# Conditioning weights: scaled in place on ScalarE, added on VectorE in operations of 2048, 1024 and 512 elements

## What is computed

```
def adaln(c, w, b):                       # w: 1024 x 6144, one per layer of the second network
    m = jax.nn.silu(c) @ w + b
    return [t[:, None, :] for t in jnp.split(m, 6, axis=-1)]
...
shift1, scale1, gate1, shift2, scale2, gate2 = adaln(c, ada_w[i], ada_b[i])
h = x * (1.0 + scale1) + shift1
```

```
g, u = jnp.split(h @ w_up, [D_FF], axis=-1)      # D_FF = 2816
g = depthwise_conv_centered(g, ffn_conv_w, ffn_conv_b)   # 3 taps
x = x + (silu(g) * u) @ w_down                   # first network
```

## Time and profile before

| what | value |
|---|---|
| median of 3 runs | 2414.7 us (2414.57 to 2418.11) |
| the profiled execution | 2417.73 us, its span 2416.0 us |
| granted PE clock, mean | 0.998 of 2.4 GHz |
| PE busy | 2392.8 us (99% of the span) |
| DVE busy | 1589.2 us (66%) |
| ACT busy | 714.3 us (30%) |
| POOL busy | 154.6 us (6%) |
| chain that ended last | PE 94%, DVE 4%, DMA 1%, issue 1% |

### The profile page before, as it was taken

One profiled execution on the slowest core, in us unless ns is written; L12 is line 12 of the kernel. 1 busy time (PEld: TensorE's weight loads), 2 busy tenths in 40 slices (PEclk: granted clock), 3 DMA queues, 4 the chain that ended last, 5 costly groups with the idle time before them and its releaser, 6 DMA issues.

```text
span 2416.0 us, 41407 instructions
## 1 busy us (share of the span) xinstructions
PE 2392.8 (99%) x17196; PEld 2180.2 (90%) x17196; DVE 1589.2 (66%) x3245; ACT 714.3 (30%) x1436; POOL 154.6 (6%) x268
## 2 busy tenths in 40 slices
PE   9999999999999999999999999999999999999998
PEld 7879999987899998999998899997889999889998
DVE  6653887566289837688744489954456984327983
ACT  3451210144312121433132233223423331443321
POOL 2000100000021000001000032021000000000000
PEclk9999999999999999999999999999999999999999
DMA  7935985574399746589454399743334555335552
GB/s 220 239 94 180 337 305 188 151 188 114 105 337 314 239 155 183 185 314 310 155 174 136 107 344 313 235 152 120 108 120 149 166 167 168 120 105 170 162 166 97
DMA packets 403269, 458.36 MB, mean 190 GB/s; under 512 B 50751, under 2 KB 374776, under 8 KB 403084
## 3 DMA queue, kind: packets, MB, share of 16 engines
q1 hardware_dynamic: 370098, 340.53, 45.2%
q0 software_dynamic: 29936, 112.73, 12.8%
q10 hardware_dynamic: 3050, 2.46, 0.4%
HBM read 451.48 MB, written 1.29 MB: 187 GB/s over the span
## 4 chain that ended last, share of the span: by engine, by line
PE 94%; DVE 4%; DMA 1%; issue 1%; ACT 0%; POOL 0%; DVEq 0%; SPq 0%; POOLq 0%; ACTq 0%
PE job_bank L994 39%; PE job_bank L1070 27%; PE job_bank L1049 11%; PE mix_bank L1049 4%; PE job_bank L1539 4%; PE mix_bank L1486 1%; PE job_bank L1514 1%; PE mix_bank L1458 1%; DVE sb_arena L2908 1%; PE mix_bank L1500 1%; PE mix_bank L1605 1%; PE mix_bank L1025 0%; PE mix_bank L1830 0%; PE job_bank L1262 0%; DVE sb_arena L2952 0%
## 5 line engine op out<-in xcount | busy, mean ns | idle before, releaser
L994 PE MATMUL job_bank<-sb_h,sb_ring 128*128 128x256 f32 x3616 | 807.1, 380 | 0.4 <-DVE sb_h L3186 0.4
L994 PEld LDWEIGHTS job_bank<-sb_h,sb_ring 128*128 128x128 f32 x3616 | 674.4, 189 | 98.9 <-issue 8.1
L2908 DVE SCALAR_TENSOR_TENSOR sb_arena<-sb_arena,sb_c_act 128x512 f32<-128x512 f32 x336 | 253.0, 753 | 10.6
L3015 DVE SCALAR_TENSOR_TENSOR sb_arena<-sb_arena,sb_par 128x256 f32<-128x256 f32 x440 | 204.4, 506 | 8.8 <-ACT sb_arena L2071 4.9
L1049 PE MATMUL job_bank<-sb_h,sb_ring 128*128 128x128 f32 x1600 | 184.1, 275 | 0.9 <-ACT sb_h L2374 0.9
L1049 PEld LDWEIGHTS job_bank<-sb_h,sb_ring 128*128 128x128 f32 x1600 | 181.2, 192 | 1.3 <-issue 1.1
L1070 PE MATMUL job_bank<-sb_t,sb_ring 128*128 128x128 f32 x1248 | 165.5, 275 | 0.0
L2071 ACT ACTIVATE sb_arena<-sb_arena,sb_par 128x256 f32<-128x256 f32 x220 | 120.2, 593 | 122.4 <-DVE sb_arena L2983 121.1
L1070 PE MATMUL job_bank<-sb_h,sb_ring 128*128 128x128 f32 x1152 | 152.8, 276 | 0.0
L1070 PEld LDWEIGHTS job_bank<-sb_t,sb_ring 128*128 128x128 f32 x1248 | 152.2, 192 | 0.0
L1070 PEld LDWEIGHTS job_bank<-sb_h,sb_ring 128*128 128x128 f32 x1152 | 144.3, 192 | 6.1 <-issue 3.3
(11 more groups left out here) (511 smaller groups left out, 3242.3 us busy)
## 6 DMA issues: line engine op xcount, KB each, us to landing
sb_arena<-in_ada_w POOLq DMA_DIRECT2D x96, 1024.0 KB, 7.4
sb_ring<-in_ffn_w_up SPq DMA_DIRECT2D x88, 1024.0 KB, 5.2
sb_ring<-in_w_up SPq DMA_DIRECT2D x44, 1024.0 KB, 6.4
sb_ring<-in_ffn_w_down SPq DMA_DIRECT2D x32, 1024.0 KB, 5.1
sb_ring<-in_w_in SPq DMA_DIRECT2D x24, 1024.0 KB, 6.2
sb_ring<-in_w_down SPq DMA_DIRECT2D x16, 1024.0 KB, 5.3
sb_ring<-in_hg_w_in SPq DMA_DIRECT2D x16, 1024.0 KB, 5.5
sb_ring<-in_ml_w_up SPq DMA_DIRECT2D x16, 1024.0 KB, 5.5
```

Source lines behind the costliest of these rows:

```text
L994: mm = pe.matmul(o, st, mv, start=(k0 + k == 0 and t == 0), stop=(k0 + k == kn - 1), skip_group_check=True)
L2908: ins = vec.scalar_tensor_tensor(out=o, in0=w, scalar=col, in1=o, op0=ALU.mult, op1=ALU.add)
L3015: ins = vec.scalar_tensor_tensor(out=o, in0=fraw[:, i % 2, v, j:j + T], scalar=pcol(column, (l * FFN_TAPS + j) * width + c), in1=o, op0=AL ...
```

## The change

Each unit is now first scaled in place by ACT: the new `ada_scale` runs four `Copy` activations of 512 elements with the column of silu(c) as their scale, and signals `ada_scaled`. ACT calls it three times in step 0 and twice in every later step, once more behind the last gate. DVE no longer multiplies: `ada_fold` adds the two scaled units of a pair (one addition of 2048 elements), `ada_add` adds the two halves of the result (1024) and then its two rows of 512. `ada_fold` stands behind the first taps, `ada_add` at the end of the step. A slot of the first unit comes free with the fold, that of the second with the last addition.

```diff
+            def ada_scale():
+                u = ada_n[0]
+                act.wait_ge(ada_in[u % ADA_RING], 16 * (u // ADA_RING + 1))
+                for k in range(4):
+                    w = ada_w[:, u % ADA_RING, k, :]
+                    col = u % 2 * 4 + k
+                    ins = act.activation(w, w, ACT.Copy, scale=c_act[:, col:col + 1])
+                ins.then_inc(s.ada_scaled, 1)
+                ada_n[0] += 1
@@ glu on ACT
                     if g[0] in fast_no:
                         keep_mid(g)
                         gate(i - 1)
+                        ada_scale()
                         keep_corner(g)
                         first_tap(stack, l, i, 0, g)
                     else:
@@
                         if i:
                             gate(i - 1)
+                        for _ in range(2 if i == 0 else 1):
+                            ada_scale()
                     if stack == 2:
                         raw_out(stack, l, i, 2, u)
                         first_tap(stack, l, i, 2)
                         if 0 < i <= KD:
                             scale_x(l, i - 1)
+                    ada_scale()
                 gate(FT // 2 - 1)
+                ada_scale()
@@ on DVE
-            def ada_half():
-                ...
-                for k in range(4):
-                    w = ada_w[:, u % ADA_RING, k, :]
-                    ...
-                        ins = vec.tensor_scalar(o, w, col, None, ALU.mult)
-                    ...
-                        ins = vec.scalar_tensor_tensor(out=o, in0=w, scalar=col, in1=o, op0=ALU.mult, op1=ALU.add)
+            def ada_fold():
+                u, first, second = ada_pair()
+                vec.wait_ge(s.ada_scaled, u + 2)
+                vec.tensor_tensor(second, first, second, ALU.add).then_inc(s.ada_acc, 1)
+
+            def ada_add():
+                u, _, w = ada_pair()
+                own(s.ada_acc, u + 1)
+                step(vec.tensor_tensor(w[:, 0:2, :], w[:, 0:2, :], w[:, 2:4, :], ALU.add))
+                settle()
+                if u + 1 >= ADA_PARTS:
+                    vec.wait_ge(s.ada_summed, (u + 1 - ADA_PARTS) // 4 + 1)
+                o = ada_part[:, u % ADA_PARTS:u % ADA_PARTS + 2, :].rearrange("p u c -> p (u c)")
+                vec.tensor_tensor(o, w[:, 0, :], w[:, 1, :], ALU.add).then_inc(s.ada_acc, 1)
+                ada_n[0] += 2
@@ glu on DVE
-                    ada_half()
                     read_out(vec, g)
                     other_taps(stack, l, i, 0)
-                    ada_half()
+                    ada_fold()
                     ...
+                    ada_add()
...
-                ada_half()
-                ada_half()
+                ada_fold()
+                ada_add()
```

More of the change, by code:

```diff
@@ L254, in __init__ @@
         self.x_scaled = sem("x_scaled")
+        self.ada_scaled = sem("ada_scaled")
 def weight_plan(a):
@@ L2887, in _, with ada_pair @@
             ada_n = [0]
-            def ada_half():
+            def ada_pair():
                 u = ada_n[0]
-                vec.wait_ge(ada_in[u % ADA_RING], 16 * (u // ADA_RING + 1))
-                first = u - u % 2
-                if u % 2 == 0 and u + 1 >= ADA_PARTS:
-                    vec.wait_ge(s.ada_summed, (u + 1 - ADA_PARTS) // 4 + 1)
-                o = ada_part[:, first % ADA_PARTS:first % ADA_PARTS + 2, :].rearrange("p u c -> p (u c)")
-                for k in range(4):
-                    w = ada_w[:, u % ADA_RING, k, :]
-                    col = c_act[:, u % 2 * 4 + k:u % 2 * 4 + k + 1]
-                    if u % 2 == 0 and k == 0:
-                        ins = vec.tensor_scalar(o, w, col, None, ALU.mult)
-                    else:
-                        if k:
-                            settle()
-                        else:
-                            own(s.ada_acc, u)
-                        ins = vec.scalar_tensor_tensor(out=o, in0=w, scalar=col, in1=o, op0=ALU.mult, op1=ALU.add)
-                    if k < 3:
-                        step(ins)
-                    else:
-                        ins.then_inc(s.ada_acc, 1)
-                ada_n[0] += 1
+                return u, ada_w[:, u % ADA_RING, :, :], ada_w[:, (u + 1) % ADA_RING, :, :]
+            def ada_fold():
[8 more added lines that the diff above has]
+                if u + 1 >= ADA_PARTS:
+                    vec.wait_ge(s.ada_summed, (u + 1 - ADA_PARTS) // 4 + 1)
+                o = ada_part[:, u % ADA_PARTS:u % ADA_PARTS + 2, :].rearrange("p u c -> p (u c)")
+                vec.tensor_tensor(o, w[:, 0, :], w[:, 1, :], ALU.add).then_inc(s.ada_acc, 1)
+                ada_n[0] += 2
             def ada_copy():
```

1 line of the change is left out of this document (added).

## The result

| kernel | median | runs | ratio to before (95%) |
|---|---|---|---|
| before | 2415.16 us | 2414.57 to 2418.11 (4) | |
| changed | 2428.04 us | 2426.78 to 2430.80 (4) | 1.0053 (1.0040 to 1.0065) |

The change costs 12.9 us at the medians; 8.8 were forecast (2423.5 us). In the last group of runs further down three executions stand far outside all the others (3538 us of the kernel before, 7261 and 8827 us of two variants); the ratios leave them out, and the medians move by 0.1 us at most without them. The profiled execution of the changed kernel took 2426.78 us, its span 2425.1, which is only 9.1 more than the span of before.

What follows compares the result with a forecast made beforehand. PE was taken to bound the kernel, busy 2392.8 of 2416.0 us. Waits of 0.5 + 2.5 + 1.6 + 2.0 + 3.2 = 9.8 us, less 1.0, gave 2414.7 + 8.8 = 2423.5 us; likeliest case 2419 to 2429, 8-in-10 range 2413.5 to 2433.

Steps and rivals of the forecast that it cites:

- first block, start: Three scalings end at 248.0 us and `keep_mid` at 248.5, where PE needs it at 247.99: a 0.5 us wait.
- second block, start: First weights land 2 us after the taps' end, so `keep_mid` ends at 690.8, PE needing it at 688.33: 2.5 us.
- second block, POOL's operations: POOL's additions slow DVE's, making the loop 16 us in two steps or so; 1.6 us reach PE.
- third block: PE waits 0.1 us for the first weight sum of g(2) and 1.9 us for `keep_mid` of g(3): together 2.0.
- fourth block: As the third, but first weights land 1.2 us after the taps' end: 1.3 + 1.9 = 3.2 us.
- these 1.6 us could double: Second block: by shared memory interfaces, POOL's slowing of DVE's additions could double its 1.6 us, making the sum 10.4.
- a wait of PE has nothing behind it that gives it back: With PE at 99%, every wait counts in full: 9.8 us more, less the 1.0 of before, +8.8 us.
- The prediction's own sign of being wrong: Wrong if PE's idle time is unchanged, waits recur in mid-block, or PE's busy time changes by more than 2 us.
- The starts are covered: Rival, chance 0.16: ACT's queue at each block's first `keep_mid` is 2 us shorter than walked; no change, 2414.7 us.
- Every second fast job is late: Rival, chance 0.16: stalls recur at g(6), g(9) and ACT waits for weights in the first two blocks; +18 us, 2433.
- a settled step is free: In the first network's settled steps, the 11.2 us loop over DVE stays under PE's 13.16 us, so they cost nothing.
- PE runs faster beside a lighter DVE: Rival, chance 0.06: 1.5 us less DVE work per step speeds matmuls by 1% of 531 us, 5.3 us; 2409.4.

Runs made afterwards that it cites:

- last group of runs: Scalings-behind-the-gate kernel with each block's third scaling put back ahead of the copy, 2421.74 us; with only two of its four operations there, 2418.95 us; before beside them, 2414.38 us.
- three kernels that take the change apart: Against the changed kernel: scalings behind the gate, 2415.57 us; no scaling on ACT, 2413.77 us; ACT scaling with DVE's old multiply-and-add operations, 2426.72 us.
- POOL late: Changed kernel with POOL's other work put behind its last issue of the conditioning weights: 2421.93 us; the same edit on the kernel before: 2413.68 us.
- DVE's part alone: Changed kernel with ACT's scalings left out; DVE waits for the weights itself and adds them unscaled: 2413.77 us, ratio 0.9998.
- the third scaling moved: Changed kernel with the third scaling of each block's first step put behind the gate of the second step: 2422.76 us, ratio 1.0035.
- the best kernel: Changed kernel with both scalings of a step behind its gate and POOL's other work behind its last weight issue: 2413.48 us, ratio 0.9996.
- those behind the gate: Changed kernel with both scalings of every step behind that step's gate on ACT (step 0, without a gate, keeps two ahead): 2415.57 us, ratio 1.0007.
- changed kernel, again: The changed kernel measured and profiled once more with no edit: 2426.08 us, ratio 1.0049 to the kernel before.

## Why the prediction was right in kind and short in size

**The mechanism** was the forecast's: ACT works in order, three scalings at a block's start and one later stand ahead of `keep_mid`, and PE waits there. The three kernels that take the change apart show it. The forecast change was 4.1 us short (8.8 against 12.9), of which a term that it didn't have makes 1.6 to 3.2, and the agreement of the stalls' sums hides errors that cancel.

**Prices.** A scaling of 0.715 us was forecast and 0.708 measured, four in 2.58 and 2.56, the fold 2.28 and 2.285, DVE 1515 and 1518 us. ACT's 960 became 946: the scalings are 244.3 us by themselves and added 232 to ACT's busy time, since each series also overlaps its neighbours (the last one above would end at 690.26, and the copy starts at 690.17). The estimate of 2.55 us for four from the Trainium skill ("ScalarE: Activation LUTs", section "What ACT_TABLE_LOAD costs") agrees with the 2.56 of the trace.

**The stalls place by place**, in us:

| place | forecast | measured | of it by POOL |
|---|---|---|---|
| first block, start | 0.5 | 0 | |
| second block, start | 2.5 | 3.2 | |
| second block, POOL's operations | 1.6 | 1.9 (0.47 + 1.47) | 1.9 |
| third block | 0.1 + 1.9 | 0 + 0.9 | |
| fourth block | 1.3 + 1.9 | 1.1 + 2.7 | 1.4 |
| sum | 9.8 | 9.8 | |

The equal sums are partly luck. At the first start twelve scalings ran in one series and took 7.45 us instead of 3 x 2.58, so that the copy ended at 248.72, as PE came to it:

```profile
240.90 7.45 ACT L2141 ACTIVATE sb_arena<-sb_arena,sb_c_act 128x512 f32<-128x512 f32 x12
248.25 0.47 ACT L2027 ACTIVATE sb_kept<-job_bank 128x384 f32<-128x384 f32 x1
```

The second start is 0.7 longer, since the third unit landed at 687.70 and ACT waited for it too. The walks of the third and fourth block were 1.0 and 0.6 us too long in their middle stall (1.9 against 0.92 and, without POOL, 1.29), and POOL's operations hit the fourth block as well, for 1.4 us that the forecast hadn't there. POOL's share is 3.35 us, twice the 1.6 of the sum. The prediction had drawn from the Trainium skill ("GPSIMD Engine Reference", section "1. Specifications") that these 1.6 us could double, since GpSimd shares memory interfaces with VectorE's two-input operations. That the operations slow each other is in the rows; the doubled size is luck, since the second block's own share was 1.9 us and the rest came in the fourth block.

**The term that was missing** is the one behind the words "a wait of PE has nothing behind it that gives it back". Nothing gave it back, but something was added: behind a stall of that length PE's clock was 0.50 for some 3.4 us, in the changed kernel's two profiles and in three others with a stall of 3.0 to 3.4 us, which cost 1.5 to 1.7 us each. Of three stalls of 2.67 to 2.75 us, two had it behind them; the one of 2.68 us in the changed kernel's first profile had not. The sum was to be 9.8 - 1.0 + 1.6 to 3.2 = 10.4 to 12.0, so 2425 to 2427 us, where 2426.1 and 2428.0 were measured. The kernel before had shown such a clock in the profile that the forecast stood on, at 966 us, in an average of 0.998 that I read as a full clock. The prediction's own sign of being wrong, a change of PE's busy time by more than 2 us, stood at 1.8 us in the first profile and at 3.8 in the second.

**The base.** The profiled execution of before lies 3 us above its median, which I took as a plain offset. Two events of that execution account for it: the half clock at 966 us (1.7), and a wait of 2.05 us at L1458 that is 0.74 us at most in the other profiles. So the 9.1 us between the spans were the wrong number to check a sum of +8.8 against; they agreed by chance.

**The rivals.** "The starts are covered" fell: the waits are in the profile. "Every second fast job is late" fell: landing took 6.1 us at the median and 15.3 at most, and no stall recurred at g(6) or g(9) of the third and fourth block. Waits did recur in the middle of the second block, at 732 and 748 us, but only beside POOL's operations: with POOL late they are gone, so a settled step is free by itself.

```profile
DMA to landing us min/median/max: 5.2/6.1/15.3
```

"PE runs faster beside a lighter DVE" fell with DVE's part alone: 71 us less on DVE and a ratio of 0.9998.

**What stays open.** Waits and clock account for 12.2 of 12.0 us in the changed kernel run again, but leave 0.5 to 2.8 us over in the other seven kernels that scale on ACT (most with the third scaling moved: 8.8 against 6.0). Part of that is how a stall is listed. The last group ahead of a stall is counted as busy to its modelled end, 0.16 us beyond the point at which the next could have started (3.62 us against a step of 3.46), and the first group behind it takes 0.99 us to the next one instead of 0.89. So a stall costs some 0.26 us more than its row says, an estimate from these rows; the seven stalls of the kernel with the third scaling moved, against one before, make 1.6 of its 2.8 us. By the same count the 12.2 us of the changed kernel become 13.5, so the good agreement there is partly luck, and about 1.5 us either way stay unexplained. PE's busy time was 2393.9 us with the third scaling moved against 2391.4 in the best kernel, with the clock at 1.00 in both; what else lengthens it wasn't tested.

## What to carry to other kernels

An engine at 26% busy still has no room at a given place: before work is put on it, walk its queue from the last thing that it waits for to the next thing that the bound engine waits for, transfers included; the same 384 operations cost 12 us with scalings in every step ahead of that point, and 1.5 us, with an interval that holds zero, with those behind the gate. Price a long stall of TensorE at more than its length when the profile's rows show a fallen clock behind one, and look for it in small windows, since the mean over a span hides it. Don't take a stall out of a list and keep the others, and don't check a forecast against a single pair of profiled spans before the events peculiar to each are known.

## What the runs showed of the hardware

- A stall of TensorE of 3.0 to 3.4 us was followed, 0.3 to 1.5 us after matmuls had resumed, by a granted clock of 0.50 for some 3.4 us, in all five profiles that had one. Two of three stalls of 2.67 to 2.75 us had it too; at the one of 2.67 us (changed kernel, again) the clock fell 0.3 us before matmuls resumed. Stalls of 1.93 us and less in the fast jobs never had it. Shortening a stall from 3.33 to 1.93 us took 2.8 us off the median, where the listed waits fell by 1.5 us.
- A DVE addition beside a POOL product of 1.97 us took 3.66 instead of 1.22 us (1024 elements) and 3.00 instead of 0.69 us (512), more than the two durations summed; beside a product of 1.09 us one of 512 elements took 2.07 us. Taking that away made no difference that can be told to the kernel before (0.3 us) and 4.15 us to the changed one.
